# A gated recurrence's gate products: from fp32 to three passes over high and low parts, with the gate weights in the weight stream

## The chip, the core and the metric

One core of a Trainium2 chip runs the whole program. The metric is the device time of one execution in microseconds; the figure shown for a kernel is the median of several executions, and one more execution is recorded by the hardware profiler. TensorE (PE in the profile) multiplies, VectorE (DVE) and ScalarE (ACT) work element by element, GpSimd (POOL) does so too and here prepares weights, SyncE (SP) issues most of the DMA transfers.

## The reference, cut to what matters

One decoder layer on 1024 tokens and 1024 channels, in fp32. One of its three parallel branches is a gated linear recurrence on 1280 channels, with gate weights in 16 diagonal blocks of 80 × 80:

```
xa = causal_conv(lru_x, conv_w, conv_b)                   # 4 taps along the tokens
gate_a = sigmoid(einsum('bsni,nij->bsnj', xb, w_a) + b_a)   # xb: xa in 16 blocks of 80 channels
gate_x = sigmoid(einsum('bsni,nij->bsnj', xb, w_x) + b_x)
log_a = -8 * gate_a * softplus(-lam);  a = exp(log_a)
u = xa * gate_x * sqrt(1 - exp(2 * log_a))
h[t] = a[t] * h[t-1] + u[t]
o_a = (h * gelu(lru_y)) @ w_lru_o
```

`lru_x` and `lru_y` are columns of the projection of the normalized input. The other branches (a delta rule over 16 heads, and windowed attention), the merge and the FFN are not touched.

## The kernel before

Activations lie transposed in SBUF, 128 channels on the partitions and 1024 tokens along them. A dense product takes its weights as a stream of blocks of 128 × 1024 numbers. SP loads block n into one of two raw buffers (`load_block`), POOL splits it into a high part (a cast to fp32r, L241) and a low part (raw minus high, L243) in one of two pairs of buffers (`split_block`), and TensorE runs three fp32r products for each k tile and token half: high × high, high × low, low × high (`three_passes`, L251). The slot of a block is its number modulo 2. A load waits for the split of the block two before it, a split for the end of the dense product two before it. The result lands in one of two PSUM pairs, by the same slot. `Block(...).before` counts the blocks ahead, and the semaphores `s_wsplit` and `s_dense` count splits and products.

The recurrence stage takes 10 channel tiles in two turns of five. In a turn the stream has ten blocks in the order `LRU_ORDER`: x0, x1, y0, x2, y1, x3, y2, x4, y3, y4. After each y block the gates of tile j are multiplied (`lru_gates`): the 80-wide blocks do not line up with tiles of 128, so a tile needs the rows of its own tile and a halo of 64 rows from each neighbour (one neighbour only for tiles 0 and 4, so 64 rows). The gate weights are loaded piece by piece by SP (L554) into the tile `gw`, as they are, and TensorE multiplies them in fp32: for each of two gates and two token halves one product of the tile's own rows (L954) and one of the halo (L955), 8 in all, each of which the profile records as two. They go to PSUM banks 4 to 7.

ScalarE copies a finished x block out of PSUM (L1411), makes the halo copy from the neighbours (L1416, L1418; two buffers in turn), takes the GELU of the y block (L1423), two sigmoids (L1425, L1426), two exponentials (L1428, L1429) and a square root (L1431), and stores the output tile. VectorE's order is written by hand: convolution of tiles 0 and 1 (L1923, L1926), four modulation products, and then for each j the gated input (L1951 minimum, L1954 and L1957 products), the convolution of tile j + 2, the scan (L1963) with the product by the GELU (L1967), and four more modulation products up to j = 2. These modulation products (`later_ada`, L1936 and L1939) are a matrix-vector product that is needed later in the layer; its weights are loaded by SP (L575) in slices of 512 KB through two buffers, four slices behind each of the blocks y1, y2, y3 and y4. Every eight of them are summed over the partitions by TensorE inside block y2 and y4 (L975) and added by VectorE (L1946); the gates that use the same PSUM bank wait for that.

Of the kernel before, what the change touches and what calls it, by code (L numbers as in the profile page):

```python
# [54 lines left out]
LRU_AT = {key: c for c, key in enumerate(LRU_ORDER)}  # L55
MOD_SH1, MOD_SC1, MOD_G1, MOD_SH2, MOD_SC2, MOD_G2, MOD_N = range(0, 56, 8)
# [7 lines left out]
STREAM = [("lora", 1, 3), ("rwkv", PAIRS, 6), ("lru", LRU_T // LRU_G, 2 * LRU_G), ("att", 1, 12),  # L64
# [61 lines left out]
def build(nc, a, out):  # L126
    ctx = ExitStack()
    with ctx:
# [144 lines left out]
        def cols(w, c0, n):  # L273
            return w[:, bass.ds(c0, n)].rearrange("(k p) m -> p k m", p=P)
# [70 lines left out]
        def bank(B, n, rows=slice(0, P)):  # L345
# [31 lines left out]
                    ("gw", LRU_G * 4 * P), ("ada", 2 * 1024), ("acc", 1024), ("halo", 2 * T)])  # L377
        LRU_ARENA = 14 * T + 8 + 20 * P + 2048 + 1024
        halo = lr["halo"].rearrange("p (s n) -> p s n", s=2)
        HALO_DONE = (1, 3, 5, 7, 8)  # L380
        l_halo = made_by("act", "lru_halo_ready")
# [9 lines left out]
        ADA_BANK = [4, 2 * Block("lru", 2 * LRU_G - 2).slot]  # L391
        s_adb = [sem(f"later_ada_weights_loaded_{k}") for k in range(2)]
        l_ev, l_sa, l_rt, l_exp = made_by("act", "lru_block_evacuated", "lru_gates_ready", "lru_root_ready", "lru_decay_ready")
        l_pe, l_ada = made_by("pe", "lru_gates_done", "ada_sums_taken")
# [121 lines left out]
        def _(sp):  # L516
# [39 lines left out]
            with sp.Fori(0, TURNS["lru"]) as g:  # L556
                for c, (kind, j) in enumerate(LRU_ORDER):
                    load_block(sp, Block("lru", c, g), cols(w_in, (COL_LX if kind == "x" else COL_LY) + j * P + g * (LRU_G * P), P), P)
# [101 lines left out]
        def _(pool):  # L660
# [31 lines left out]
            split_turns("lru", [1024] * (2 * LRU_G))  # L692
# [22 lines left out]
        def _(pe):  # L715
# [225 lines left out]
            def lru_gates(g, j):  # L941

                pe.wait_ge(l_cv, upto(g * (4 * LRU_G) + 4 * min(j + 2, LRU_G)))
                pe.wait_ge(l_sa, upto(g * (2 * LRU_G) + 2 * j))
                pe.wait_ge(v_post, upto(PAIRS * POST))
                pe.wait_ge(ada_out, upto(g * ADA_U + (ADA_OUT0 + j // 2)))
                n = 2 * 16 * len(PIECES_OF[j])
                pe.wait_ge(s_gw[j], g * n + n)
                pe.wait_ge(l_halo, upto(g * HALO_DONE[-1] + HALO_DONE[j]))
                rows = slice(0 if j + 1 < LRU_G else 64, P if j > 0 else 64)  # L950
                for q in range(2):
                    for h in range(2):
                        hs = slice(h * 512, (h + 1) * 512)
                        mm(ps[:, 4 + 2 * q + h, :], gw[:, j, q, 0, :], xa_t[:, j, hs], start=True, stop=False)  # L954
                        ins = mm(ps[:, 4 + 2 * q + h, :], gw[rows, j, q, 1, :], halo[rows, j % 2, hs], start=False, stop=True)  # L955
                ins.then_inc(l_pe, 1)

            with pe.Fori(0, TURNS["lru"]) as g:
                for c, (kind, j) in enumerate(LRU_ORDER):
                    pe.wait_ge(l_ev, upto(g * len(LRU_ORDER) + max(c - 1, 0)))  # L960
                    if c == 0:
                        pe.wait_ge(ada_out, upto(g * ADA_U + ADA_OUT0))
                    if c == 1:
                        pe.wait_ge(a_gate, upto(PAIRS * 3))

                    def later_sums(k):

                        if k == 4:
                            pe.wait_ge(ada_acc, upto(g * ADA_G + (ADA_ACC0 + ADA_PHASE * j)))
                            if j == 2:  # L970
                                pe.wait_ge(l_sa, upto(g * (2 * LRU_G) + 2 * j))
                            else:
                                pe.wait_ge(l_ev, upto(g * len(LRU_ORDER) + c))
                            for q in range(8):
                                ins = mm(ps[:, ADA_BANK[j // 2 - 1], q:q + 1], ada_acc1[:, q * P:(q + 1) * P], ones[:, 0:1], start=True, stop=True)  # L975
                            ins.then_inc(l_ada, 1)
                    dense(pe, Block("lru", c, g), after=later_sums if kind == "y" and j in (2, 4) else None)
                    if kind == "y":
                        lru_gates(g, j)
# [299 lines left out]
        def _(act):  # L1279
# [122 lines left out]

            for g in range(TURNS["lru"]):
                for c, (kind, j) in enumerate(LRU_ORDER):
                    blk = Block("lru", c, g)
# [7 lines left out]
                    act.wait_ge(l_pe, upto(g * LRU_G + max(j - 1, 0)))  # L1413
                    act.wait_ge(l_cv, upto(g * (4 * LRU_G) + 4 * min(j + 2, LRU_G)))
# [9 lines left out]
                    act.wait_ge(l_pe, upto(g * LRU_G + (j + 1)))  # L1424
# [6 lines left out]
                    fn(lr["a2"], lr["a2"], ACT.Sqrt, scale=-1.0, bias=one_b).then_inc(l_rt, 1)  # L1431

# [229 lines left out]
        def _(dve):  # L1662
# [254 lines left out]
            def conv(g, j):  # L1917
# [4 lines left out]
                dve.wait_ge(l_pe, upto(g * LRU_G))  # L1922
# [35 lines left out]

            def recur(g, j):
# [11 lines left out]
            for g in range(TURNS["lru"]):  # L1971
                conv(g, 0)
                conv(g, 1)
                later_ada(g, 0)
                for j in range(LRU_G):
                    gated_input(g, j)
                    if j == 3:
                        later_ada_add(g, 1)
                    if j + 2 < LRU_G:
                        conv(g, j + 2)  # L1980
                    if g * LRU_G + j == LRU_T - 1:
                        dve.wait_ge(l_pe, upto(LRU_T))
# [271 lines left out]
```

## Time and profile before

| | us |
|---|---|
| median of 3 executions | 2933.76 (2930.98 to 2934.75) |
| the profiled execution | 2931.37 |
| its span, first to last instruction | 2929.4 |
| TensorE busy in the span | 2843.5 (97%) |
| VectorE, POOL, ScalarE busy | 1424.1, 752.5, 742.0 |
| mean granted TensorE clock | 0.992 of full speed |

A profile gives each instruction's start and duration on its engine, and what ended the idle time before it. Matmuls overlap, so the duration of one is longer than its step; steps are read from the chain. The times in the timelines count from the start of the span. A line number is that of kernel.py.

### The profile page before, as it was taken

To read this page: it belongs to the slowest core of one execution; us is meant where nothing else is said; L and a number is where in the kernel's file an instruction comes from. 1 tells how busy PE (TensorE), PEld (TensorE's weight loads), DVE (VectorE), ACT (ScalarE), POOL (GpSimd) and SP (SyncE) were. 2 spreads that over 40 slices of the span, in tenths; PEclk is the share of its full clock that TensorE was granted. 3 is DMA by queue.
4 is the path that set the end of the run, shared out by engine and by line. 5 is a ranking of instruction groups with operands and counts; after the bars stand their busy time and mean duration, and the time that the engine had idled before them with its cause. 6 is when DMAs were issued, how large, how long until landed. Compare 5 with 4: busy or idle time off the path is not lost.

```text
span 2929.4 us, 60683 instructions
## 1 busy us (share of the span) xinstructions
PE 2843.5 (97%) x25747; PEld 2350.4 (80%) x25747; DVE 1424.1 (49%) x1549; ACT 742.0 (25%) x1077; POOL 752.5 (26%) x490
## 2 busy tenths in 40 slices
PE   4999999999999999999999998999999999999999
PEld 3797979888888888867777776888888888888887
DVE  5645554546464545565654556566654222222223
ACT  4312121313131212144455666011122000000001
POOL 0403040303031212122222111333333333333332
PEclk9999999999999999999999999999999999999999
DMA  5201020202010111142431101476311111111112
GB/s 193 77 25 58 20 70 9 75 16 63 25 54 25 54 31 38 48 135 84 132 90 39 60 32 69 130 230 195 113 44 57 44 50 50 46 47 50 50 43 79
DMA packets 222611, 201.34 MB, mean 69 GB/s; under 512 B 22369, under 2 KB 193467, under 8 KB 222395
## 3 DMA queue, kind: packets, MB, share of 16 engines
q1 hardware_dynamic: 208928, 150.70, 17.1%
q10 hardware_dynamic: 13467, 47.31, 4.4%
q8 instruction: 191, 3.13, 0.4%
q14 instruction: 25, 0.20, 0.0%
HBM read 167.57 MB, written 30.41 MB: 68 GB/s over the span
## 4 chain that ended last, share of the span: by engine, by line
PE 94%; DVE 2%; issue 1%; ACT 1%; DMA 1%; SPq 0%; POOL 0%; ACTq 0%; DVEq 0%; POOLq 0%
PE ps L251 68%; PE ps L860 3%; PE ps L874 3%; PE ps L871 2%; PE ps L838 2%; PE ps L955 1%; PE ps L954 1%; PE ps L923 1%; PE ps L1049 1%; PE ps L828 1%; DMA arena<-in_w_ada 1%; PE ps L1074 1%; PE ps L1062 1%; PE ps L794 1%; PE ps L909 1%
## 5 line engine op out<-in xcount | busy, mean ns | idle before, releaser
L251 PE MATMUL ps<-x_hi,w_hi 128*128 128x512 f32 (+1 forms) x2576 | 835.2, 398 | 7.2 <-issue 4.1
L251 PE MATMUL ps<-x_lo,w_hi 128*128 128x512 f32 (+1 forms) x2576 | 815.6, 391 | 0.0
L251 PE MATMUL ps<-x_hi,w_lo 128*128 128x512 f32 (+1 forms) x2576 | 815.2, 391 | 0.0
L241 POOL CAST w_hi<-w_raw 128x1024 fp32r<-128x1024 f32 (+2 forms) x221 | 210.1, 951 | 2117.4 <-PE ps L251 1487.1
L251 PEld LDWEIGHTS ps<-x_hi,w_hi 128*128 128x128 f32 (+1 forms) x2576 | 477.9, 188 | 129.7 <-issue 30.7
L251 PEld LDWEIGHTS ps<-x_hi,w_lo 128*128 128x128 f32 (+1 forms) x2576 | 483.9, 188 | 104.7
L251 PEld LDWEIGHTS ps<-x_lo,w_hi 128*128 128x128 f32 (+1 forms) x2576 | 484.2, 188 | 100.8
L243 POOL TENSOR_TENSOR w_lo<-w_raw,w_hi 128x1024 fp32r<-128x1024 f32 (+2 forms) x221 | 484.0, 2190 | 17.7
L2203 DVE TENSOR_TENSOR arena<-ps,arena 128x1024 f32<-128x1024 f32 x21 | 25.7, 1225 | 376.5 <-PE ps L251 376.5
L251 PE MATMUL ps<-hid,w_hi 128*128 128x512 f32 x704 | 188.7, 390 | 0.0
L2221 DVE SCALAR_TENSOR_TENSOR arena<-ps,mod,arena 128x1024 f32<-128x1024 f32 x88 | 113.0, 1284 | 128.3 <-PE ps L251 128.2
L251 PEld LDWEIGHTS ps<-hid,w_hi 128*128 128x128 f32 x704 | 131.7, 188 | 27.0
L1868 DVE COPY_PREDICATED arena<-hid,ps 128x256 f32<-128x256 int32 x144 | 72.1, 501 | 137.7 <-PE ps L871 87.6
L1646 ACT ACTIVATE hid<-arena 128x1024 fp32r<-128x1024 f32 x22 | 23.4, 1062 | 442.0 <-PE ps L251 316.9
L251 PE MATMUL ps<-hid,w_lo 128*128 128x512 f32 x352 | 108.4, 389 | 0.0
L1497 ACT ACTIVATE arena<-arena 128x256 f32<-128x256 f32 x128 | 75.4, 590 | 80.5 <-DVE arena L2046 80.5
L874 PE MATMUL ps<-arena 64*64 64x64 f32 x2560 | 89.0, 218 | 0.0
L860 PE MATMUL ps<-arena 64*64 64x64 f32 x2560 | 84.1, 218 | 0.8
L874 PEld LDWEIGHTS ps<-arena 64*64 64x64 f32 x2560 | 83.0, 135 | 0.0
L860 PEld LDWEIGHTS ps<-arena 64*64 64x64 f32 x2560 | 79.9, 135 | 1.7 <-issue 1.7
L251 PEld LDWEIGHTS ps<-hid,w_lo 128*128 128x128 f32 x352 | 66.1, 188 | 13.8
L1765 DVE TENSOR_TENSOR arena<-arena 128x1024 f32<-128x1024 f32 (+1 forms) x27 | 41.8, 1548 | 72.6 <-ACT arena L1314 71.5
(289 smaller groups left out, 3449.2 us busy)
## 6 DMA issues: line engine op xcount, KB each, us to landing
w_raw<-in_w_in SPq DMA_DIRECT2D x78, 512.0 KB, 3.9
arena<-in_w_ada SPq DMA_DIRECT2D x48, 512.0 KB, 4.7
w_raw<-in_w_ffn_in SPq DMA_DIRECT2D x44, 512.0 KB, 3.7
arena<-gates_sig ACTq DMA_DIRECT2D x40, 512.0 KB, 4.2
gates_sig<-arena ACTq DMA_DIRECT2D x24, 512.0 KB, 2.7
w_raw<-in_w_ffn_out SPq DMA_DIRECT2D x22, 512.0 KB, 3.5
arena<-in_x SPq DMA_DIRECT2D x16, 512.0 KB, 6.9
y_a<-arena ACTq DMA_DIRECT2D x10, 512.0 KB, 2.6
```

The lines of the kernel that those rows point to most:

```text
L241: nc.gpsimd.tensor_copy(hi, raw).then_inc(s_whi, 1)
L243: nc.gpsimd.tensor_tensor(lo, raw, hi.bitcast(F32), ALU.subtract).then_inc(s_wsplit, 1)
L251: ins = nc.tensor.matmul(dst[h], wp, xp[h], start=first and m == 0, stop=last and m == 2)
L794: ins = mm(ps[hp, 4, c:c + 1], rw["bv"][hp, c * CHUNK:(c + 1) * CHUNK], ones[hp, 0:1], start=True, stop=True)
L838: ins = mm(dst, src[hp, c * CHUNK:(c + 1) * CHUNK], ar[hp, c, :, :], start=True, stop=True)
L860: ins = mm(bank(B, 2, hp)[:, c % BATCH, :], am[hp, c, AM_BA, :], xx[hp, 0, c, :], start=True, stop=True)
L871: ins = mm(bank(B, 0, hp)[:, c % BATCH, :], xx[hp, 1, c, :], y1[hp, c, :], start=True, stop=True)
L874: ins = mm(bank(B, 1, hp)[:, c % BATCH, :], y1[hp, c, :], xx[hp, 1, c, :], start=True, stop=True)
L1497: fn(sc[:, h, nn, :], sc[:, h, nn, :], ACT.Exp, bias=sm[:, SM_NEG, h, nn:nn + 1], scale=rq[:, gg % 2, t, n0 + nn, h:h + 1], accum_out=sm[: ...
L1765: v.tensor_tensor(dst, x0, x1, ALU.subtract).then_inc(v_mix, 1)
L1868: v.copy_predicated(blocks_of(xx[:, o, batch(B), :], lv, o), level_mask(lv, o), blocks_of(bank(B, o), lv, o)).then_inc(v_xu, 1)
L2221: v.scalar_tensor_tensor(r, ps[:, at:at + 2, :], mod[:, MOD_G2 + m:MOD_G2 + m + 1], r, ALU.mult, ALU.add).then_inc(m_dn, 1)
```

## The change

The gate products become three-pass products like the dense ones.

- The gate weights of a tile become blocks of the stream: one block of 512 columns behind each of y0 to y3, and two of 256 columns (gate a, gate x) behind y4, so that a turn has 16 blocks. POOL splits them from `gw` (`split_gates`). SP, in place of a load, waits until the block two before is split and then counts up the semaphore of the slot.
- The tile's own rows and its halo are each kept as a high part, made by ScalarE (`own_high`, and the lower halo rows in the loop), and a low part, made by VectorE (`low`). They lie in the four quarters of `hid`, the FFN's tensor, one set for all tiles. The arena loses its halo buffers.
- A gate product of a tile is 24 fp32r matmuls where it was 8 fp32 ones.
- As the slots of the stream shift, an x or y block can have the same PSUM pair as the block multiplied just before; it then waits for the copy of that block instead of the one before it.

```diff
+LRU_STREAM = [key for kind, j in LRU_ORDER
+              for key in [(kind, j)] + ([] if kind == "x" else [("gates", j)] if j + 1 < LRU_G else [("gate_a", j), ("gate_x", j)])]
+LRU_BLOCK = {key: c for c, key in enumerate(LRU_STREAM)}
...
+        own_hi, own_lo, halo_hi, halo_lo = (hid[:, k * T:(k + 1) * T] for k in range(4))
+        PARTS_DONE = (2, 5, 8, 11, 13)
...
+        def gates_before(g, j):
+            return lru_block("x", 0, g).before if j == 0 else lru_block("gates", j - 1, g).before + 1 if j < LRU_G else lru_block("gate_x", j - 1, g).before + 1
...
# SP
-                        sp.wait_ge(l_pe, upto(g * LRU_G))
+                        sp.wait_ge(s_dense, upto(gates_before(g, 0)))
                         wait_alone(sp)
                         load_gate_weights(g, j)
+                        for key in (("gates",) if j + 1 < LRU_G else ("gate_a", "gate_x")):
+                            blk = lru_block(key, j, g)
+                            sp.wait_ge(s_wsplit, upto(blk.before - 1))
+                            wait_alone(sp)
+                            sp.sem_inc(s_w[blk.slot], 16)
                     if c in (4, 6, 8, 9):
                         first = ADA_PHASE * (4, 6, 8, 9).index(c)
...
# POOL
+            def split_gates(g, key, j):
+                blk = lru_block(key, j, g)
+                q = slice(1, 2) if key == "gate_x" else slice(0, 1) if key == "gate_a" else slice(0, 2)
+                raw = gw[:, j, q, :, :].rearrange("p q h m -> p (q h m)")
+                hi, lo = (t[:, blk.slot, 0:raw.shape[1]] for t in (w_hi, w_lo))
+                n = 2 * 16 * len(PIECES_OF[j])
+                pool.wait_ge(s_gw[j], g * n + n)
+                pool.wait_ge(s_dense, upto(blk.before - 1))
+                wait_alone(pool)
+                nc.gpsimd.tensor_copy(hi, raw).then_inc(s_whi, 1)
+                pool.wait_ge(s_whi, upto(blk.before + 1))
+                nc.gpsimd.tensor_tensor(lo, raw, hi.bitcast(F32), ALU.subtract).then_inc(s_wsplit, 1)
...
# TensorE, lru_gates
-                pe.wait_ge(l_cv, upto(g * (4 * LRU_G) + 4 * min(j + 2, LRU_G)))
+                pe.wait_ge(l_low, upto(g * PARTS_DONE[-1] + PARTS_DONE[j]))
...
                 for q in range(2):
-                    for h in range(2):
-                        hs = slice(h * 512, (h + 1) * 512)
-                        mm(ps[:, 4 + 2 * q + h, :], gw[:, j, q, 0, :], xa_t[:, j, hs], start=True, stop=False)
-                        ins = mm(ps[:, 4 + 2 * q + h, :], gw[rows, j, q, 1, :], halo[rows, j % 2, hs], start=False, stop=True)
-                ins.then_inc(l_pe, 1)
+                    blk = lru_block("gates" if j + 1 < LRU_G else ("gate_a", "gate_x")[q], j, g)
+                    if j + 1 == LRU_G or q == 0:
+                        pe.wait_ge(s_wsplit, upto(blk.before + 1))
+                        wait_alone(pe)
+                    at = 0 if j + 1 == LRU_G else 2 * P * q
+                    dst = [ps[:, 4 + 2 * q + h, :] for h in range(2)]
+                    three_passes(dst, [t[:, blk.slot, at:at + P] for t in (w_hi, w_lo)], (both(own_hi), both(own_lo)), True, False)
+                    ins = three_passes(dst, [t[rows, blk.slot, at + P:at + 2 * P] for t in (w_hi, w_lo)], (both(halo_hi, rows), both(halo_lo, rows)), False, True)
...
-                    pe.wait_ge(l_ev, upto(g * len(LRU_ORDER) + max(c - 1, 0)))
+                    same = c > 0 and lru_block(*LRU_ORDER[c - 1]).slot == lru_block(kind, j).slot
+                    pe.wait_ge(l_ev, upto(g * len(LRU_ORDER) + (c if same else max(c - 1, 0))))
...
# ScalarE
+            def own_high(g, j):
+                act.wait_ge(s_dense, upto(gates_before(g, j)))
+                act.wait_ge(l_cv, upto(g * (4 * LRU_G) + 4 * (j + 1)))
+                fn(own_hi, xa_t[:, j, :], ACT.Copy).then_inc(l_high, 1)
+                if j > 0:
+                    fn(halo_hi[64:128, :], xa_t[64:128, j - 1, :], ACT.Copy).then_inc(l_high, 1)
...
                     if j + 1 < LRU_G:
-                        fn(halo[0:64, j % 2, :], xa_t[0:64, j + 1, :], ACT.Copy).then_inc(l_halo, 1)
-                    if j > 0:
-                        fn(halo[64:128, j % 2, :], xa_t[64:128, j - 1, :], ACT.Copy).then_inc(l_halo, 1)
+                        act.wait_ge(s_dense, upto(gates_before(g, j)))
+                        act.wait_ge(l_cv, upto(g * (4 * LRU_G) + 4 * (j + 2)))
+                        fn(halo_hi[0:64, :], xa_t[0:64, j + 1, :], ACT.Copy).then_inc(l_high, 1)
...
                     fn(lr["a2"], lr["a2"], ACT.Sqrt, scale=-1.0, bias=one_b).then_inc(l_rt, 1)
+                    if j + 1 < LRU_G:
+                        own_high(g, j + 1)
...
# VectorE
+            def low(g, j, part):
+                n = g * PARTS_DONE[-1] + (PARTS_DONE[j - 1] if j > 0 else 0) + (part if j > 0 else part // 2) + 1
+                hi, lo, rows, src = ((own_hi, own_lo, slice(0, P), j), (halo_hi, halo_lo, slice(64, P), j - 1), (halo_hi, halo_lo, slice(0, 64), j + 1))[part]
+                dve.wait_ge(l_high, upto(n))
+                v.tensor_tensor(lo[rows, :], xa_t[rows, src, :], hi[rows, :].bitcast(F32), ALU.subtract).then_inc(l_low, 1)
...
                 conv(g, 1)
+                low(g, 0, 0)
+                low(g, 0, 2)
                 later_ada(g, 0)
                 for j in range(LRU_G):
                     gated_input(g, j)
                     if j == 3:
                         later_ada_add(g, 1)
+                    if j + 1 < LRU_G:
+                        low(g, j + 1, 0)
+                        low(g, j + 1, 1)
                     if j + 2 < LRU_G:
                         conv(g, j + 2)
+                        low(g, j + 1, 2)
```

## Rows read from the trace of the kernel before

**Rows 1.** The page's chain that ended last, shares of the span by engine

```profile
PE 94%; DVE 2%; issue 1%; ACT 1%; DMA 1%; SPq 0%; POOL 0%; ACTq 0%; DVEq 0%; POOLq 0%
```

**Rows 2.** Windows: us; busy PE, PEld, DVE, ACT, POOL (instructions); clock; DMA; GB/s

```profile
1204.70:1516.98 312.28, 312.28 (x1245) 225.01 (x1241) 192.26 (x133) 141.62 (x126) 82.81 (x42) 1.00 0.36 111
```

**Rows 3.** Chain in order of time, first turn: start us, us, what

```profile
1216.78 32.66 PE ps L251 x144
1249.44 0.86 PE ps L954 x2
1250.30 1.05 PE ps L955 x2
...
1257.68 22.01 PE ps L251 x96
1279.69 0.86 PE ps L954 x2
...
1286.56 17.73 PE ps L251 x78
1304.29 1.68 PE ps L975 x16
```

**Rows 4.** Timeline of SP's DMA issues, first turn

```profile
1235.72 0.39 SPq L233 DMA_DIRECT2D w_raw<-in_w_in  x1
...
1241.93 8.11 SPq L575 DMA_DIRECT2D arena<-in_w_ada  x4
```

**Rows 5.** The modulation loads' line (L575), 1190 to 1540 us

```profile
DMA to landing us min/median/max: 3.3/3.9/5.8
```

**Rows 6.** Timeline of VectorE, modulation products before gates 0

```profile
1246.37 0.75 DVE L1936 TENSOR_SCALAR arena<-arena,mod 128x1024 f32<-128x1024 f32 x1
...
1250.73 4.80 DVE L1939 SCALAR_TENSOR_TENSOR arena<-arena,mod 128x1024 f32<-128x1024 f32 x2 [1.25 <-DMA arena<-in_w_ada]
```

**Rows 7.** Timeline of VectorE, between gates 0 and gates 1

```profile
1262.33 0.69 DVE L1951 TENSOR_SCALAR arena<-arena 128x1024 f32<-128x1024 f32 x1 [6.81 <-ACT arena L1428]
...
1270.76 5.94 DVE L1926 SCALAR_TENSOR_TENSOR arena<-arena,lru_par 128x1024 f32<-128x1024 f32 x3
1276.62 2.28 DVE L1963 TENSOR_TENSOR_SCAN arena<-arena 128x1024 f32<-128x1024 f32 x1
```

**Rows 8.** Timeline of ScalarE, GELU, table load and root of tile 0

```profile
1249.48 1.02 ACT L1423 ACTIVATE arena<-ps 128x1024 f32<-128x1024 f32 x1 [0.57 <-PE ps L251]
...
1263.36 1.28 ACT L1431 ACT_TABLE_LOAD   x1
1264.66 1.15 ACT L1431 ACTIVATE arena<-arena,bias_t 128x1024 f32<-128x1024 f32 x1
```

**Rows 9.** Timeline of POOL, the split of one whole block

```profile
1249.60 1.04 POOL L241 CAST w_hi<-w_raw 128x1024 fp32r<-128x1024 f32 x1 [6.88 <-issue]
1250.72 2.34 POOL L243 TENSOR_TENSOR w_lo<-w_raw,w_hi 128x1024 fp32r<-128x1024 f32 x1
```

**Rows 10.** Timeline of POOL, the split of the next turn's first block

```profile
1351.07 2.70 POOL L243 TENSOR_TENSOR w_lo<-w_raw,w_hi 128x1024 fp32r<-128x1024 f32 x1
```

**Rows 11.** Timeline of VectorE, the same stretch

```profile
1351.46 3.39 DVE L1954 TENSOR_TENSOR arena<-arena 128x1024 f32<-128x1024 f32 x1
```

**Rows 12.** One line: VectorE's convolution steps, ns min/median/max

```profile
L1926 DVE SCALAR_TENSOR_TENSOR arena<-arena,lru_par x30: 1283/1285/3304, 1229.8 to 1484.8; 128x1024 f32<-128x1024 f32 x30
```

**Rows 13.** One line: VectorE's low parts of the first stage

```profile
L1729 DVE TENSOR_TENSOR x_lo<-arena,x_hi x8: 1214/1215/1225, 48.7 to 72.4; 128x1024 fp32r<-128x1024 f32 x8
```

**Rows 14.** One line: ScalarE's high parts in the FFN

```profile
L1646 ACT ACTIVATE hid<-arena x22: 1057/1062/1063, 2228.0 to 2895.9; 128x1024 fp32r<-128x1024 f32 x22
```

**Rows 15.** Groups of POOL by form: xcount | busy us, mean ns

```profile
L243 POOL TENSOR_TENSOR w_lo<-w_raw,w_hi 128x512 fp32r<-128x512 f32 x56 | 73.0, 1304 | 4.5
```

**Rows 16.** Windows in the attention stage around an idle TensorE

```profile
1626.80:1629.80 3.00, 3.00 (x8) 1.94 (x6) 1.02 (x1) 2.97 (x10) 0.00 (x0) 0.50 0.00 0
```

**Rows 17.** Timeline of the kernel, 1300 to 1320 us

```profile
1308.87 0.17 DVE L1946 TENSOR_TENSOR mod<-ps,mod 128x8 f32<-128x8 f32 x1
```

More of the change, by code:

```diff
@@ L61 @@
 C_KEEP = C_ATT
-STREAM = [("lora", 1, 3), ("rwkv", PAIRS, 6), ("lru", LRU_T // LRU_G, 2 * LRU_G), ("att", 1, 12),
+STREAM = [("lora", 1, 3), ("rwkv", PAIRS, 6), ("lru", LRU_T // LRU_G, len(LRU_STREAM)), ("att", 1, 12),
           ("oa0", 4, 2), ("oa1", 4, 2), ("oa2", 4, 2), ("oc0", 4, 2), ("oc1", 4, 2), ("ob0", 4, 2), ("ob1", 4, 2),
@@ L376, in build, with lru_block @@
         lr = carve([("xp", T + 8), ("xa", LRU_G * T), ("ga", T), ("gx", T), ("aa", T), ("a2", T), ("gy", T), ("ya", T),
[L377 to L381, printed above, removed]
+                    ("gw", LRU_G * 4 * P), ("ada", 2 * 1024), ("acc", 1024)])
+        LRU_ARENA = 12 * T + 8 + 20 * P + 2048 + 1024
+        own_hi, own_lo, halo_hi, halo_lo = (hid[:, k * T:(k + 1) * T] for k in range(4))
+        PARTS_DONE = (2, 5, 8, 11, 13)
+        l_high, l_low = made_by("act", "lru_operand_high"), made_by("dve", "lru_operand_low")
+        def lru_block(kind, j, g=0):
+            return Block("lru", LRU_BLOCK[kind, j], g)
+        def gates_before(g, j):
+            return lru_block("x", 0, g).before if j == 0 else lru_block("gates", j - 1, g).before + 1 if j < LRU_G else lru_block("gate_x", j - 1, g).before + 1
         ada_w1 = lr["ada"].rearrange("p (s m) -> p s m", s=2)
@@ L390, in build @@
         ADA_U = ADA_G // KT
-        ADA_BANK = [4, 2 * Block("lru", 2 * LRU_G - 2).slot]
+        ADA_BANK = [4, 2 - 2 * lru_block("y", LRU_G - 1).slot]
         s_adb = [sem(f"later_ada_weights_loaded_{k}") for k in range(2)]
         l_ev, l_sa, l_rt, l_exp = made_by("act", "lru_block_evacuated", "lru_gates_ready", "lru_root_ready", "lru_decay_ready")
-        l_pe, l_ada = made_by("pe", "lru_gates_done", "ada_sums_taken")
+        l_ada = made_by("pe", "ada_sums_taken")
         l_cv, l_sq, l_u, l_out, l_z, gw_zero = made_by(
@@ L557, in _ @@
                 for c, (kind, j) in enumerate(LRU_ORDER):
-                    load_block(sp, Block("lru", c, g), cols(w_in, (COL_LX if kind == "x" else COL_LY) + j * P + g * (LRU_G * P), P), P)
+                    load_block(sp, lru_block(kind, j, g), cols(w_in, (COL_LX if kind == "x" else COL_LY) + j * P + g * (LRU_G * P), P), P)
                     if c == 1:
@@ L691, in _ @@
                         nc.gpsimd.tensor_copy(rw["xx"].rearrange("p (c n) -> p c n", n=CHUNK), eye.unsqueeze(1).broadcast_to([P, 2 * CHUNKS, CHUNK])).then_inc(x_id, 1)
-            split_turns("lru", [1024] * (2 * LRU_G))
+            def split_gates(g, key, j):
[10 more added lines that the diff above has]
+                nc.gpsimd.tensor_tensor(lo, raw, hi.bitcast(F32), ALU.subtract).then_inc(s_wsplit, 1)
+            with pool.Fori(0, TURNS["lru"]) as g:
+                for key, j in LRU_STREAM:
+                    if key in ("x", "y"):
+                        split_block(pool, lru_block(key, j, g), 1024)
+                    else:
+                        split_gates(g, key, j)
             for c in range(PER["att"]):
@@ L976, in later_sums @@
                             ins.then_inc(l_ada, 1)
-                    dense(pe, Block("lru", c, g), after=later_sums if kind == "y" and j in (2, 4) else None)
+                    dense(pe, lru_block(kind, j, g), after=later_sums if kind == "y" and j in (2, 4) else None)
                     if kind == "y":
@@ L1401, in store_y @@
                 act.dma_start(y_a[n * P:(n + 1) * P, :], lr["ya"]).then_inc(s_ya, 16)
+            def own_high(g, j):
[4 more added lines that the diff above has]
+                    fn(halo_hi[64:128, :], xa_t[64:128, j - 1, :], ACT.Copy).then_inc(l_high, 1)
             for g in range(TURNS["lru"]):
                 for c, (kind, j) in enumerate(LRU_ORDER):
-                    blk = Block("lru", c, g)
+                    blk = lru_block(kind, j, g)
                     lp = lambda row: lru_par[:, bass.ds(g * LRU_G + (row + j), 1)]
@@ L1978, in _ @@
                         later_ada_add(g, 1)
+                    if j + 1 < LRU_G:
+                        low(g, j + 1, 0)
+                        low(g, j + 1, 1)
                     if j + 2 < LRU_G:
                         conv(g, j + 2)
+                        low(g, j + 1, 2)
                     if g * LRU_G + j == LRU_T - 1:
-                        dve.wait_ge(l_pe, upto(LRU_T))
+                        dve.wait_ge(s_dense, upto(Block("att", 0).before))
                         for n in range(2):
```

14 lines of the change are left out of this document (7 added, 7 removed).

## Prediction

> **What bounds the kernel now.** I read the chain that ended last first: TensorE is 94% of it [rows 1]. The change touches only the recurrence stage, so next came the windows of that stage: from 1204.7 to 1517.0 TensorE is busy for all of 312.28 us, VectorE 192, POOL 83 [rows 2]. So one microsecond off the gates is one off the end, as long as nobody keeps TensorE waiting, and each new wait is paid in full. In the chain in order of time the reader is to see the cycle of a tile j: gates j, block x(j+2), block y(j+1), gates j+1, with no gap [rows 3]. Then the timelines of SP, VectorE, ScalarE and POOL inside one cycle show how early each input of the next gates is [rows 4 to 9]. That is where this change will be decided.
>
> **What TensorE saves.** The gates of a middle tile take 1286.56 − 1279.69 = 6.87 us; those of an end tile, where 64-row and 128-row products alternate, 1257.68 − 1249.44 = 8.24 (1.05 a step for 0.86) [rows 3]. Three-pass products go at 32.66/144 = 0.227 us in the blocks x0, x1, y0 [rows 3]. After: 24 of them, 5.44 us. An end tile changes between 64 and 128 rows 4 times instead of 8; at 0.19 each (taken from the fp32 row, from 0 to 0.4 if it is another price in this mode), 6.2. Also the two blocks behind fp32 gates take 22.01, where 96 × 0.227 = 21.77 [rows 3]; that 0.25 goes. A turn saves 3 × 1.43 + 2 × 2.04 + 5 × 0.25 = 9.6, two turns 19 us.
>
> **What is added elsewhere.** ScalarE: where it copied halo halves (1.06 a copy) it now makes high parts; the new one is a copy of the tile itself, 1.06 by the same form elsewhere [rows 14]. VectorE: two low parts for tile 0, three for 1 to 3, two for 4, a subtraction of the form that took 1.21 [rows 13]: 13 a turn, 16 us. POOL: six more splits a turn, the subtraction of 512 columns at 1.30 [rows 15] and a cast of half a whole one's, half that again for the last two. None of this is on TensorE, and VectorE has 120 us free. What counts is where the additions stand in its order.
>
> **Three dependencies that get longer.** (a) The gates now have one set of high and low tensors, so part j+1 is made only after gates j. (b) Blocks are split two ahead in a ring of two. With gate blocks in the ring, "two ahead" is less time. (c) SP waits, before it hands gate block j to POOL, for the split of the block two positions earlier, and everything behind it in SP's order waits too: the four modulation loads behind y1, y2, y3, y4. VectorE multiplies these in its fixed order before it starts on the gates' results.
>
> **Gates 1, worked through.** Before, SP issued the modulation loads at 1241.93 [rows 4], and the fourth product ended at 1250.73 + 4.80 = 1255.53 [rows 6], well before the exponential that releases VectorE at 1262.33 [rows 7, 8]. Now SP waits for the split of x2. This starts when y0 ends (1249.4) and takes 1.04 + 2.34 [rows 9] and some 0.2 of gaps: 1253.0, loads out from 1253.7. By the same 13.6 us from first issue to last product VectorE is free at 1267.3; as the loads go two in flight at 3.9 us (3.3 to 5.8) [rows 5] and POOL's split of y1 falls among the products, I take 1268.4. Without this, the earlier end of the gates would have released it at 1260.2. From there: minimum 0.7 [rows 7], a collision with POOL's subtraction for gate block 1 1.2, root 1.2 [rows 8], then product and two low parts at 1.2 each: 1275.2 (ScalarE's two copies behind the root keep pace). Convolution of x2: 0.8 + 3 × 1.28 without POOL [rows 12]; before, its three steps took 5.94 because the split of a whole block fell on them [rows 7]; now only the cast for x3 does, about 5.8: 1281.0. Copy on ScalarE 1.15: 1282.1. The last low part then meets POOL's subtraction for x3 and ends at 1284.5. TensorE, with gates 0 done at 1249.4 + 6.2 and 21.8 for two blocks, is ready at 1277.4. **Wait 7.1 us.**
>
> Collisions: while POOL subtracted from 1351.07 for 2.70 us, a VectorE product, 1.21 by the form of [rows 13], took 3.39 [rows 10, 11]; it ended 1.1 after POOL did. So each takes turns for a whole instruction. The Trainium skill, page "SBUF — State Buffer", section "Who interferes with whom", says the same of VectorE operations with two SBUF inputs: whoever issues first holds the port pair. By that rule the low parts, two SBUF inputs each, are among those that can be held up; if they were not, gates 1 would start near 1283.3. The trace has no subtraction into this tensor beside POOL.
>
> **The other waits of a turn.** Block x3 now has the PSUM pair that y1 has just left, so it waits for the GELU of y1, which waits for the output of tile 0: gates 1 start + scan 2.3 [rows 7] and product 1.2, store issue and gaps 0.5, table load 1.3 and GELU 1.0 [rows 8] = 6.3 against 5.44: **0.8**; the same behind gates 3, **0.8**. Gates 2: modulation loads leave at 1284, right after x3's split; the fourth product ends about 1297.5; then 6.1 to the end of two low parts (no collision this time), 6.4 of convolution (a gate block's split falls on it) and 2.5 of copy and low part give 1312.5 or a little more, and gates 2 also wait for the modulation sum, which VectorE adds after scan and product of tile 1: 1316.5 to 1317.5. TensorE is ready at 1314.2 (y2 holds the 1.68 of sums [rows 3]): **3.2**. Gates 3: loads wait for the split of x4, so for y2's end, then POOL collides with scan and product of tile 1; out at 1320.3, products done at 1335, then 16.5 as for gates 1: 1351.7 against 1344.6, **7.1**. Gates 4: low parts behind the modulation sum, **1.0** in two pieces. The next block: gate x alone lasts 3.1, a whole split 3.4 and its gaps start only when gate a is done and meet VectorE: **1.6**. Sum 7.1 + 0.8 + 3.2 + 7.1 + 0.8 + 1.0 + 1.6 = 21.6 a turn, 43.2 in two.
>
> **Sum.** 43.2 − 19 = +24. The profiled execution took 2931.4 (span 2929.4 and 2.0 around it): 2955.6. The median shown is 2.4 above it: 2958.
>
> **Clock.** Behind idle time of 1.9 us in the attention stage TensorE ran at a granted 0.50 (1.2 GHz, not 2.4) for the 3 us from 1626.8 [rows 16]. Waits of 7 us will do this too: four in all, each costing half of 3 us or a little more, 6 to 7 together. The gates after a wait are slower then, but in the cycle behind gates 1 VectorE is held by the loads (1297.5) and not by the exponential (1294.6), and the PSUM wait of 0.8 is absorbed. I take 0 for it, up to +7. The Trainium skill, page "TensorE: Matmul & The Clock Gate", section "HAM oscillation — how this bites in real kernels", has waits re-throttle the array each time; by it the sum would be the upper one.
>
> **Rivals.**
> 1. The forecast: loads late and parts late, 2958. If nothing collides with POOL and loads land at 3.3, gates 1 and 3 start 3 us sooner, four times: −12, 2946; if they land at 5.8 and the clock costs 7, +13, 2971. Chance 0.78.
> 2. Larger still: each late load also pushes the next whole cycle, so the waits do not stay at 7 but grow as the weight loads queue behind them; 8 waits with 2 us more, 2972 or more. Against it: SP issued the load of y1 at 1235.7 for a block that began at 1268 [rows 4], and a load that goes 10 us later still comes in time. Chance 0.09.
> 3. The modulation data is there in time (SP's wait passes early, or VectorE's products fit in). Then VectorE starts at 1260.2, conv(x2) at 1267.6 when its block is copied, last low part by 1276, in front of 1277.4. Waits left: 0.8 + 3.2 + 0.8 + 1.0 + 1.6 = 7.4 a turn, 15 in all: −4, 2930. It decides if the loads go out before 1246. The order in the code and the ring speak against it. Chance 0.08.
> 4. Everything hidden, the other side: 2934 − 19 = 2915. The mechanism is the shorter gates alone, decisive if each part is ready within the 21.8 us of two blocks. For it: before, no gates waited. Against: VectorE's add for gates 2 was done at 1309.0 for a start at 1310.2 [rows 17], and 5 us of work moves in front of it. Chance 0.05.
>
> **Range and chances.** A difference under 0.2% (5.9 us) can't be told from none. Rival 1 is slower throughout its range; rival 3 lies within 0.2% mostly, with a third of it faster. Slower 0.87, same 0.06, faster 0.07. The range leaves out rivals 3 and 4 and most of 2: 2943 to 2972.
>
> **What would show it.** Right: gates start-to-start cycles of about 35 us for 30; TensorE idle before gates 1 and 3 ended by VectorE's low-part subtraction; SP's modulation loads at 1253 and not at 1242; products ending near 1268; gates of 5.4 us; conv of x2 at 1275. The modulation step is wrong if those loads leave before 1246, the collisions if conv takes 4.7 throughout, the saving if 24 gate products take other than 5.4 us at full clock. The prediction falls if gates 1 start by 1278.

## The result, and the profile after

| | before | after |
|---|---|---|
| median of 4 executions each, us | 2932.61 (2930.98 to 2934.75) | 2952.59 (2951.24 to 2957.77) |
| ratio of after to before, 95% interval | | 1.0077 (1.0064 to 1.0089) |
| the profiled execution, us | 2931.37 | 2951.54 (span 2949.7) |
| TensorE busy in the span, us | 2843.5 | 2835.1 |
| mean granted TensorE clock | 0.992 | 0.987 |

The kernel is 20 us slower. TensorE is busy for 8 us less and still ends 20 later, and the page's chain that ended last shows where the rest went (it was 94% TensorE, [rows 1]):

```profile
PE 89%; DVE 4%; DMA 2%; issue 2%; ACT 1%; POOL 1%; SPq 0%; ACTq 0%; POOLq 0%; DVEq 0%
```

To compare kernels I use one measure from here on, called the stage: from the first matmul of block x0 to the first transpose of the attention stage, both from TensorE's timeline. Before it lasts 1216.53 to 1527.94, 311.4 us, and TensorE is busy in all of it. After, the windows view (columns as in [rows 2]) says this of it, and of the 9 us behind the start of gates 1:

```profile
1215.38:1548.30 332.92, 304.05 (x1316) 245.58 (x1314) 217.47 (x163) 156.49 (x141) 110.48 (x66) 0.95 0.34 104
```
```profile
1283.20:1286.00 2.80, 2.77 (x7) 2.22 (x8) 2.77 (x2) 0.00 (x0) 0.00 (x0) 0.50 0.95 323
1286.00:1289.00 3.00, 3.00 (x9) 2.33 (x8) 2.69 (x3) 2.35 (x3) 0.00 (x0) 0.57 0.58 221
1289.00:1292.00 3.00, 3.00 (x15) 2.45 (x14) 0.49 (x2) 1.74 (x2) 0.38 (x1) 1.00 0.78 224
```

The stage is 21.5 us longer, which is the whole difference. It holds 332.92 − 304.05 = 28.9 us in which TensorE is idle, and its granted clock is 0.95 where it was 1.00: right behind the wait at gates 1 it is 0.50 (1.2 GHz) and comes back to 2.4 GHz some 5 us later. TensorE's timeline, first turn, has every wait with what ended it in brackets:

```profile
1283.23 2.04 PE L255 MATMUL ps<-hid,w_hi 128*128 128x512 f32 x4 [6.86 <-DVE hid L2017]
...
1315.51 1.17 PE L255 MATMUL ps<-hid,w_hi 128*128 128x512 f32 x4 [0.44 <-DVE mod L1998]
...
1350.00 2.05 PE L255 MATMUL ps<-hid,w_hi 128*128 128x512 f32 x4 [7.03 <-DVE hid L2017]
...
1373.56 1.16 PE L255 MATMUL ps<-hid,w_hi 128*128 128x512 f32 x4 [0.55 <-POOL w_lo L722]
...
1376.93 0.50 PE L255 MATMUL ps<-x_hi,w_hi 128*128 128x512 f32 x1 [0.16 <-POOL w_lo L247]
```

These are gates 1, 2, 3, the second half of gates 4, and the next block: 15.0 us in this turn, 13.8 in the second. L2017 is the low-part subtraction, L1998 the modulation sum. The reader is also to see the first column of durations: four matmuls take 2.04 at gates 1 and 3 and 1.17 at gates 2, the clock again.

Back from gates 1 along the inputs, first SP's queue (answers to [rows 4]: the modulation loads, there at 1241.93):

```profile
1235.78 4.41 SPq L237 DMA_DIRECT2D w_raw<-in_w_in  x2
...
1252.41 8.17 SPq L593 DMA_DIRECT2D arena<-in_w_ada  x4
```

then VectorE (to [rows 6, 7]): modulation products, minimum, low parts, convolution of x2, last low part.

```profile
1256.48 2.15 DVE L1988 TENSOR_SCALAR arena<-arena,mod 128x1024 f32<-128x1024 f32 x1 [10.00 <-DMA arena<-in_w_ada]
...
1266.05 1.29 DVE L1991 SCALAR_TENSOR_TENSOR arena<-arena,mod 128x1024 f32<-128x1024 f32 x1 [2.14 <-DMA arena<-in_w_ada]
1267.27 1.78 DVE L2003 TENSOR_SCALAR arena<-arena 128x1024 f32<-128x1024 f32 x1
...
1271.49 2.47 DVE L2017 TENSOR_TENSOR hid<-arena,hid 128x1024 fp32r<-128x1024 f32 x2
...
1274.84 4.58 DVE L1978 SCALAR_TENSOR_TENSOR arena<-arena,lru_par 128x1024 f32<-128x1024 f32 x3
1280.61 2.10 DVE L2017 TENSOR_TENSOR hid<-arena,hid 64x1024 fp32r<-64x1024 f32 x1 [1.18 <-ACT hid L1468]
```

and POOL's subtraction for block x3, beside that last low part:

```profile
1278.42 3.20 POOL L247 TENSOR_TENSOR w_lo<-w_raw,w_hi 128x1024 fp32r<-128x1024 f32 x1
```

The 64-row low part takes 2.10 us and ends 1.09 after POOL does; where nothing runs beside it, it takes 1.22 (below). VectorE sat 10.00 us before the first modulation product, for the load.

### The profile page after: what moved, and what is told of

Read it like the earlier page. It is cut to its first block, busy times and chain, and to the rows that moved or that the text cites. A ratio compares the mean times of both kernels' runs of the same rounds, so it can differ in the third digit from the quotient of the medians.

```text
span 2949.7 us, 60983 instructions
## 1 busy us (share of the span) xinstructions
PE 2835.1 (96%) x25827; PEld 2371.9 (80%) x25827; DVE 1449.8 (49%) x1575; ACT 752.0 (25%) x1087; POOL 782.2 (27%) x514
## 4 chain that ended last, share of the span: by engine, by line
PE 89%; DVE 4%; DMA 2%; issue 2%; ACT 1%; POOL 1%; SPq 0%; ACTq 0%; POOLq 0%; DVEq 0%
PE ps L255 66%; PE ps L897 3%; PE ps L911 3%; DMA arena<-in_w_ada 2%; PE ps L908 2%; PE ps L875 2%; PE ps L960 1%; PE ps L1091 1%; PE ps L865 1%; PE ps L1116 1%; PE ps L1104 1%; DVE arena L1978 1%; PE ps L831 1%; DVE hid L2017 1%; PE ps L917 1%
## 5 line engine op out<-in xcount | busy, mean ns | idle before, releaser
L255 PE MATMUL ps<-hid,w_hi 128*128 128x512 f32 (+1 forms) x864 | 239.7, 400 | 28.5 <-DVE hid L2017 26.6
L255 PEld LDWEIGHTS ps<-hid,w_hi 128*128 128x128 f32 (+1 forms) x864 | 164.5, 193 | 69.0 <-issue 35.3
L255 PE MATMUL ps<-hid,w_lo 128*128 128x512 f32 (+1 forms) x432 | 135.7, 396 | 0.0
L255 PEld LDWEIGHTS ps<-hid,w_lo 128*128 128x128 f32 (+1 forms) x432 | 82.8, 192 | 17.8
```

The lines of the kernel that those rows point to most:

```text
L255: ins = nc.tensor.matmul(dst[h], wp, xp[h], start=first and m == 0, stop=last and m == 2)
```

## Experiments

Every ratio is to executions of the kernel before on the same chip: their median was 2934.0 beside e1 to e4, 2934.2 beside e5 to e7 and 2933.1 beside e10 and e11. The stage and its idle time are from each kernel's own trace, so from one execution; that of e1 was the longest of its ten (2940.5), that of e3 the shortest of its four (2943.0). What a kernel differs from before by its stage and by its medians agrees within some 5 us.

| kernel | median us | ratio to before, 95% interval | stage us | TensorE idle in it | clock in it |
|---|---|---|---|---|---|
| before | 2932.6 | | 311.4 | 0 | 1.00 |
| after | 2952.6 | 1.0077 (1.0064 to 1.0089) | 332.9 | 28.9 | 0.95 |
| e1_loads_first | 2932.4 | 0.9996 (0.9987 to 1.0006) | 314.9 | 11.0 | 0.97 |
| e2_late_loads_only | 2938.8 | 1.0021 (1.0011 to 1.003) | 317.3 | 5.5 | 1.00 |
| e3_no_low_parts | 2948.0 | 1.0054 (1.0035 to 1.0072) | 324.5 | 19.3 | 0.97 |
| e4_gates_short_only | 2917.1 | 0.9937 (0.9916 to 0.9959) | 293.9 | 0 | 1.00 |
| e5_early_sum | 2925.7 | 0.9978 (0.9967 to 0.999) | 307.4 | 6.4 | 0.98 |
| e6_early_sum_ring4 | 2921.8 | 0.9958 (0.9946 to 0.997) | 298.3 | 2.7 | 1.00 |
| e7_clock_kept | 2950.1 | 1.0056 (1.0035 to 1.0076) | 331.9 | 10.9 | 1.00 |
| e10_before_new_order | 2931.8 | 0.9996 (0.9986 to 1.0005) | 311.4 | 0 | 1.00 |
| e11_ring4_only | 2949.8 | 1.0058 (1.0041 to 1.0075) | 329.6 | 22.4 | 0.96 |

**Loads first: is it SP's order?** In the kernel after, SP's hand-over of the gate block, with its wait for the split of the block two positions earlier, moves behind the four modulation loads. Nothing else changes.

```diff
                         load_gate_weights(g, j)
-                        for key in (("gates",) if j + 1 < LRU_G else ("gate_a", "gate_x")):
-                            blk = lru_block(key, j, g)
-                            sp.wait_ge(s_wsplit, upto(blk.before - 1))
-                            wait_alone(sp)
-                            sp.sem_inc(s_w[blk.slot], 16)
                     if c in (4, 6, 8, 9):
...
                             sp.dma_start(ada_w1[:, n % 2, :], src).then_inc(s_adb[n % 2], 16)
+                    if kind == "y":
+                        for key in (("gates",) if j + 1 < LRU_G else ("gate_a", "gate_x")):
+                            blk = lru_block(key, j, g)
+                            sp.wait_ge(s_wsplit, upto(blk.before - 1))
+                            wait_alone(sp)
+                            sp.sem_inc(s_w[blk.slot], 16)
```

> The changed kernel with one edit: SP issues the four modulation loads behind y1 to y4 before it waits for the split of the block two ahead of the gate block, not behind that wait. Theory (late modulation loads cost most of the waits): first loads of a turn leave near 1241 to 1247 and not 1252, the wait before gates 1 (6.9 us in the changed kernel) is gone, the one before gates 3 (7.0) falls by half or more, and the time falls by 12 to 18 us, to about 2937. Rival A (the low parts and POOL's splits are what is late, the loads only share the blame): the waits stay at 4 us and more, 2948. Rival B (nothing but the loads was late): the whole 19 us that TensorE saves appears, 2915.

Measured: 2932.4, level with before, where I had expected 2937; by the medians the 20 us are gone, in the stage 18.0 of the 21.5. The loads leave at

```profile
1252.30 7.88 SPq L588 DMA_DIRECT2D arena<-in_w_ada  x4
```

in a trace in which x0 starts 5.7 later than in that of after (1221.09 for 1215.38), so 5.8 us earlier in the stage. The waits of 6 to 7 us at gates 1 and 3 are gone. What is left, from TensorE's timeline:

```profile
1314.60 1.51 PE L255 MATMUL ps<-hid,w_hi 128*128 128x512 f32 x4 [3.29 <-DVE mod L1999]
...
1358.11 2.04 PE L1018 MATMUL ps<-keep,arena 128*128 128x1 f32 x15 [1.94 <-DVE arena L1992]
```

Gates 2 wait for the modulation sum, and TensorE's sums for the last modulation product. So first loads that leave 5.8 us later cost 18 us of stage, because four cycles are hit. All of that is idle time (28.9 us for 11.0); TensorE's busy time is the same in both (304.05 and 303.96), so the slow clock has no part in the difference.

The loads are not back where they were before. They leave 37.0 us behind x0 after, 31.2 in e1 and 25.4 before. Of the 5.8 that are left, 5.2 are in the load of block y1, which stands ahead of them in SP's queue: it goes out 24.4 us behind x0 in both new kernels and 19.2 before. In e1 it goes out at 1245.50, just behind POOL's split of gate block 0 (1243.96 + 1.30): the ring of two, point (b) of the prediction.

**Late loads alone: is it enough?** The kernel before, with one wait in SP's order ahead of the modulation loads, for the split of the block just issued, so that they leave at about the time they do after.

```diff
                     if c in (4, 6, 8, 9):
                         first = ADA_PHASE * (4, 6, 8, 9).index(c)
+                        sp.wait_ge(s_wsplit, upto(Block("lru", c, g).before + 1))
+                        wait_alone(sp)
```

> The kernel before, with fp32 gates, and one wait more: SP lets the modulation loads behind y1 to y4 go only when that block itself is split, which is the moment at which the changed kernel lets them go. Theory: the late loads alone make VectorE late; gates 1 start 1 to 3 us late, the stage grows by 8 to 15 us, 2941 to 2948. Rival A (loads are hidden when there are no low parts behind them): no change, 2933.

Measured: 2938.8, and loads at 1253.21, 36.9 us behind x0 as in the kernel after. I had expected a wait at gates 1 and 8 to 15 us of stage; it is 5.9. There are waits at gates 2 only, 2.9 and 2.6 us in the two turns; gates 1 and 3 do not wait:

```profile
1312.82 1.12 PE L956 MATMUL ps<-arena 128*128 128x512 f32 x2 [2.87 <-DVE mod L1948]
```

Loads that are 11.5 us later than before cost 5.9 us of stage where nothing else is longer; with the rest of the change, the last 5.8 of them alone cost 18 (e1). The lateness needs the rest of the change beside it. My reading is that low parts, shorter gates and late loads eat from the same slack; no run has late loads and short gates without the other additions.

**No low parts.** The kernel after, with no low-part subtraction on VectorE; the gates use the high part in its place, with the same 24 products.

```diff
-                pe.wait_ge(l_low, upto(g * PARTS_DONE[-1] + PARTS_DONE[j]))
+                pe.wait_ge(l_high, upto(g * PARTS_DONE[-1] + PARTS_DONE[j]))
...
-                    three_passes(dst, [t[:, blk.slot, at:at + P] for t in (w_hi, w_lo)], (both(own_hi), both(own_lo)), True, False)
...
+                    three_passes(dst, [t[:, blk.slot, at:at + P] for t in (w_hi, w_lo)], (both(own_hi), both(own_hi)), True, False)
...
-                    if j + 1 < LRU_G:
-                        low(g, j + 1, 0)
-                        low(g, j + 1, 1)
```

> The changed kernel without VectorE's low-part subtractions: TensorE multiplies the high part where it would multiply the low part, with the same number of products, so the output lacks the low parts. Loads stay late. Theory: 2.5 us before the convolution and 2.1 to 3.3 behind it leave the path to gates 1 and 3, the waits there fall from 7 to about 4, 2941 to 2944. Rival B (loads are the whole cause): the waits stay, within 3 us of the changed kernel, 2950. Rival A (low parts are the whole cause): waits gone, 2915 to 2920.

Measured: 2948.0. The waits at gates 1 and 3, 6.0 to 7.0 us after, fall to some 4.2 as expected, and end on ScalarE's high halo part (behind the same convolution). The time did not fall as expected (2941 to 2944). The stage gives 8.4 us back, somewhat under half of what the loads gave in e1 (18.0); by the medians it is 4.6 of 20. So the low parts are an addition to a chain that is late already, worth 5 to 8 us.

**Gates short, nothing else.** The kernel before; its gate products become 24 three-pass ones on operands that lie there anyway (lg0 by x), so that nobody has anything more to prepare.

```diff
+                part = lambda t, r: [t[r, 0, h * 512:(h + 1) * 512] for h in range(2)]
...
-                        mm(ps[:, 4 + 2 * q + h, :], gw[:, j, q, 0, :], xa_t[:, j, hs], start=True, stop=False)
-                        ins = mm(ps[:, 4 + 2 * q + h, :], gw[rows, j, q, 1, :], halo[rows, j % 2, hs], start=False, stop=True)
...
+                    three_passes(dst, [lg0_hi, lg0_lo], (part(x_hi, whole), part(x_lo, whole)), True, False)
+                    ins = three_passes(dst, [lg0_hi[rows, :], lg0_lo[rows, :]], (part(x_hi, rows), part(x_lo, rows)), False, True)
```

> The kernel before, with its gates as 24 three-pass products whose operands are tensors that lie ready (a weight tensor of the stage before, the first tile of the input), so the gate values are not those of the reference; all waits and copies are those of before. It measures what TensorE saves by itself. Theory: 5.4 us for a middle tile, 6.2 for an end tile, 19 us less in all, 2914. Rival (a shorter gate alone already uncovers a wait, as VectorE's modulation sum for gates 2 had only 1.2 us to spare): 2917 to 2922.

Measured: 2917.1; the stage falls by 17.5 us without a wait. The time is that of my rival, but not for its reason: nothing was uncovered, the saving was smaller. That is the most that the change could have brought.

**The order of VectorE and the buffers.** e5 is e1, and VectorE takes the first modulation sum before the scan of tile 1 rather than behind it. e6 is e5 with four buffers for the modulation weights where there were two (two semaphores of the first stage are counted on for the two new ones).

```diff
+                    if j == 1:
+                        later_ada_add(g, 0)
                     recur(g, j)
-                    if j == 1:
-                        later_ada_add(g, 0)
...
-                            sp.wait_ge(ada_acc, upto(g * ADA_G + (ADA_ACC0 + n - 1)))
+                            sp.wait_ge(ada_acc, upto(g * ADA_G + (ADA_ACC0 + n - 3)))
...
-                            sp.dma_start(ada_w1[:, n % 2, :], src).then_inc(s_adb[n % 2], 16)
+                            sp.dma_start(ada_w1[:, n % 4, :], src).then_inc(s_adb[n % 4], 16)
```

> The kernel after with SyncE's loop of hand-over waits behind the modulation loads, and VectorE's modulation sum and next products ahead of the scan of the block, not behind it. Loads_first alone stood at 2932.4 us (ratio 0.9996), with a wait of 3.3 us at gates 2 that ended on the modulation sum. If that wait is VectorE's order of work alone, it goes (3.3 us in each turn) and this kernel stands 2 to 6 us under loads_first, 2926 to 2930. If it is the ring of two loads that limits, the wait moves to the next low parts or to the sum's taking by TensorE, at the same total: 2930 to 2935. My estimate is the second: the products wait for loads that are issued only as their buffers come free.

> As early_sum, with four buffers in place of two for the modulation weights, so that loads run four products ahead. If loads paced by two buffers are what is left of the waits, the idle time of TensorE in the stage falls from 11 us (loads_first) to under 6, with the slow clock that follows each stop, and the time is 2920 to 2928 us, under both kernels. If VectorE's own work is what paces, it stays at 2930 to 2935.

Measured: e5 2925.7, e6 2921.8. For e5 I had taken the second reading (the wait only moves) and was wrong: the wait at gates 2 is gone, and the sums wait 1.7 and 1.5, much as in e1 (1.9 and 1.4). e6 came out as its first reading said: idle time 2.7 us, clock 1.00 for the stage. It stands 12 us under the kernel before on the same chip. Its stage, and its last low part before gates 1, at 1.22 us with nothing of POOL's beside it:

```profile
1215.79:1514.04 298.25, 295.52 (x1315) 239.60 (x1314) 229.92 (x163) 156.47 (x141) 120.39 (x66) 1.00 0.37 116
```
```profile
1273.88 1.22 DVE L2019 TENSOR_TENSOR hid<-arena,hid 64x1024 fp32r<-64x1024 f32 x1 [1.19 <-ACT hid L1470]
```

**The same order, without the change.** e10 is the kernel before with e6's four buffers and early sum.

> The kernel before, with what early_sum_ring4 adds to VectorE's and SyncE's side: four buffers for the modulation weights and the first modulation sum ahead of the scan. The gate products stay fp32. It tells whether the 12 us that early_sum_ring4 stands under before come from the change or from the schedule alone. In the trace of before TensorE doesn't wait for the modulation in this stage, so I expect no change: 2931 to 2937 us, ratio 0.999 to 1.001. Rival: the earlier loads and sum give something on their own; then it is under 2928, and the change itself is worth less than the two together.

Measured: 2931.8, stage 311.4 as before. The new order is worth nothing by itself, since no wait was there to remove; e6's gain is the change's own.

**Four buffers alone.** e11 is the kernel after with the four buffers, SP's order and the sum left as they are.

> The kernel after with four buffers in place of two for the modulation weights, and nothing else: SyncE's loads still stand behind its wait for the split of the gate weights, and the sum stands where it was. If the place in SyncE's queue is the cause of the waits of 6 to 7 us at gates 1 and 3, the loads still leave at about 1252; what four buffers save is the pacing between them (products end at about 1263 in place of 1267), so the waits fall to 3 or 4 us and the time to 2938 to 2945. If the two buffers were the cause, it stands where early_sum_ring4 does, 2919 to 2925. If neither, at 2950 to 2955.

Measured: 2949.8. The wait at gates 1 fell more than I had written, the total less: it is 0.2 us short of my third case, "neither". TensorE's timeline of the first turn:

```profile
1276.91 1.15 PE L255 MATMUL ps<-hid,w_hi 128*128 128x512 f32 x4 [1.39 <-DVE hid L2018]
...
1311.76 1.91 PE L255 MATMUL ps<-hid,w_hi 128*128 128x512 f32 x4 [4.38 <-DVE mod L1999]
...
1357.88 1.44 PE L1018 MATMUL ps<-keep,arena 128*128 128x1 f32 x6 [3.81 <-DVE arena L1992]
```

The loads still leave at 1251.55 but all within 2.4 us; gates 1 wait 1.4 for 6.9, gates 2 wait 4.4 for 0.4, gates 3 not at all for 7.0, and the sums 3.8 for none. A wait taken away at one place came back at the next. e6 has these four buffers and no such waits, but two things more, SP's order and the early sum; no run parts those two with four buffers.

**The clock.** e7 is the kernel after with 26 more fp32r products ahead of TensorE's wait at gates 1 and 3, into a bank that nobody reads then; they fill the wait.

```diff
+                pe.wait_ge(l_sa, upto(g * (2 * LRU_G) + 2 * j))
+                if j in (1, 3):
+                    for _ in range(26):
+                        mm(ps[:, 7, :], lg0_hi, x_hi[:, 0, 0:512], start=True, stop=True)
                 pe.wait_ge(l_low, upto(g * PARTS_DONE[-1] + PARTS_DONE[j]))
-                pe.wait_ge(l_sa, upto(g * (2 * LRU_G) + 2 * j))
```

> The kernel after, with 26 extra fp32r products of 128x512 (lg0 high by the high part of x, into a bank that nobody reads then) ahead of TensorE's wait for the low parts at gates 1 and gates 3. They fill some 5.9 us of waits of 6.0 to 7.0 and change nothing that anyone waits for. Theory: the stop costs twice, once as the wait and once as the clock of 0.50 behind it; with the engine busy in the wait, gates 1 and 3 take 5.4 us in place of 8.1, so up to 4 x 2.6 = 10 us off: 2943 us, ratio to before 1.003 to 1.004. Rival: what comes behind gates 1 and 3 waits for VectorE all the same, so that most of it is given back as longer waits at gates 2 and at the sums: 2949 to 2953. I expect 2944 to 2947.

Measured: 2950.1. The clock stays at 1.00 and gates 1 take 5.7 us in place of 8.1, but the total is near that of after, as the rival said and against my own 2944 to 2947:

```profile
1281.24 1.17 PE L255 MATMUL ps<-hid,w_hi 128*128 128x512 f32 x4 [0.25 <-DVE hid L2020]
...
1287.36 0.72 PE L255 MATMUL ps<-x_hi,w_hi 128*128 128x512 f32 x2 [0.40 <-ACT arena L1476]
...
1312.64 1.16 PE L255 MATMUL ps<-hid,w_hi 128*128 128x512 f32 x4 [1.39 <-DVE mod L2001]
...
1348.35 0.93 PE L255 MATMUL ps<-hid,w_hi 128*128 128x512 f32 x3 [2.36 <-DVE hid L2020]
```

Counted from x0's start, gates 2 begin 1.6 us earlier than after and gates 3 only 0.4 (98.5 for 100.1, 134.3 for 134.6). TensorE arrives sooner and waits longer. The 0.40 at block x3 is the PSUM wait of the prediction, which the slow gates of the kernel after had covered.

## Why the prediction held, step by step

The forecast was +24 us and 2958; measured +20.0 and 2952.6. In the stage: forecast −19.2 + 43.2 = +24.0; measured +21.5. It comes apart as follows, e6 giving the busy time of the same products at full clock (295.5): saving 311.4 − 295.5 = 15.9; slow clock 304.05 − 295.5 = 8.5; idle 28.9; −15.9 + 8.5 + 28.9 = +21.5. So the direction and the cause were right. The total is nearer than its terms: the long waits came 1.8 us under the forecast and the small ones 12.6, the clock 8.5 over and the saving 3.3 short. That these leave 2.5 us is in part luck.

- **The chain to gates 1.** x0 starts 1.15 us earlier in the trace of after (1215.38 for 1216.53), so 1.15 is added to compare. Loads leave: forecast 1253.7, measured 1253.6. VectorE free: 1268.4, measured 1268.4. Two low parts done: 1275.2, measured 1275.1. Convolution done: 1281.0, measured 1280.6. Last low part: 1284.5, measured 1283.9, the gates 0.5 behind it. TensorE ready: 1277.4, measured 1277.5. Wait: 7.1, measured 6.9. Gates 3: start 1351.7, measured 1351.2; wait 7.1, measured 7.0. Second turn 6.0 and 6.8. These terms carry the forecast, and e1 shows that the loads' place behind SP's hand-over is what makes them: with that alone undone, the waits at gates 1 and 3 are gone and the time is that of before.
- **The small waits (7.4 a turn)** came to 1.2 in the first turn and 1.1 in the second. These are the terms most off. Gates 2 start at 1316.7 in the terms of before, forecast 1316.5 to 1317.5, so VectorE's side was right; but TensorE, held by slow gates 1, was ready only 0.4 ahead, not 3.2. The PSUM waits of 0.8 are covered in the same way. e7, where the clock is kept, tells how much the slow gates covered: there the small waits are 3.6 and 3.5 us, so 4.8 of the 12.6. The other 7.8 were too much in any case: gates 2 wait 1.4 in e7 for 3.2, the PSUM pairs 0.40 for 0.8. The next block waited 0.16 and 0.20 for 1.6: I put the splits of the two half blocks too close to it. With the long ones, 26.6 for 28.4, the waits came to 28.9 in two turns, not 43.2.
- **The clock, taken at 0 with up to +7,** cost 8.5 of TensorE's busy time. As an entry of the sum it was mis-sized, but the reason given for 0 (VectorE is held anyway, so slower gates are absorbed) holds for most of it: e7 takes the slow clock away and gets 1.0 us of stage back, as the waits grow by almost as much (by the medians 2.5, from ranges that touch). So part of "clock 8.5" and of "small waits 12.6 less than forecast" are the same microseconds: the forecast counted the small waits at full clock and the clock at nothing, and each is off in part by what the other covers. The rule cited from the Trainium skill, page "TensorE: Matmul & The Clock Gate", section "HAM oscillation — how this bites in real kernels", is borne out as far as the clock goes: it fell at each of the four long waits. Its consequence for the time, the upper sum, is not.
- **The saving, 19,** was 15.9 in the full change and 17.5 with products alone (e4). Gates 0 took 6.21 (forecast 6.2), middle gates 5.4 at full clock. The 0.25 for each of ten changes of mode is what isn't there: 17.5 less the 16.7 of the gates leaves 0.8 for all ten. The prediction had read 22.01 for the two blocks behind gates 0, where rows change between 64 and 128; behind gates 2 the chain of before has 21.81. The other 1.6 between e4 and e6 lies in pieces of 0.06 to 0.2 at gates 1, 3 and 4 and in the blocks behind them (gates 1 take 5.50 us in e6 and 5.44 in e4).
- **Collisions.** The last low part took 2.10 beside POOL's subtraction and 1.22 without. The minimum took 1.78 beside the one for gate block 1 and 0.69 in e1, where it comes elsewhere. The rule of the Trainium skill, page "SBUF — State Buffer", section "Who interferes with whom", held for a subtraction that writes hid: it ended 1.09 us after POOL's, as the product of [rows 11] did (1.1). In both, POOL had started first.
- **Rivals.** The larger one (2972 or more) did not come: waits do not grow from cycle to cycle. The third (modulation data in time, 2930) did not come either; e1 comes near it at 2932.4, with loads that leave at 1247.7 in the terms of before and 11.0 us of waits for 15. The fourth (2915, everything hidden) is what e4 shows for the gates alone at 2917.1; e6 comes to 2921.8.

Open: how much of after's wait at gates 1 goes to each collision by itself, as no run removes POOL's split alone. Also open are the 5.2 us by which the load of y1 goes out late in both new kernels, as no run has a longer ring; and two sets of high and low parts, so that tile j+1's are made a tile earlier, weren't tried.

## What to carry to other kernels

A wait put in a queue is a wait for everything behind it: before pricing "SP waits for the split", list the loads issued after it and who consumes them. Here moving four loads of each group ahead of a hand-over was worth 20 us, and turned a change that costs 0.8% into one that, with the sum taken earlier and two more buffers, brings 0.4%. And when the engine that sets the end gets shorter work, re-time all its suppliers; taking one wait away (e11, e7) mostly uncovers the next.

## What the runs showed of the hardware

The length of a wait didn't decide what the clock did. In the stage of e5, a wait of 1.45 us ahead of the sums was followed by full clock for 2 us and 0.54 in the next 2, while TensorE was busy throughout:

```profile
1495.40:1497.40 2.00, 1.97 (x17) 1.97 (x18) 1.85 (x3) 1.39 (x2) 0.00 (x0) 1.00 0.00 0
1497.40:1499.40 2.00, 2.00 (x6) 1.57 (x7) 2.00 (x3) 1.76 (x2) 0.00 (x0) 0.54 0.00 0
```

In e11, a wait of 1.39 us ahead of gates 1 was followed by 1.00 in both stretches:

```profile
1276.90:1279.00 2.10, 2.09 (x9) 1.78 (x10) 2.06 (x2) 0.00 (x0) 2.10 (x1) 1.00 0.00 0
1279.00:1281.00 2.00, 2.00 (x10) 1.65 (x9) 1.59 (x1) 0.00 (x0) 1.92 (x2) 1.00 0.00 0
```

and in e2, whose gate products are fp32, a wait of 2.87 us was followed by 1.00 in each 2 us up to 1320.8. The low clock can also come some 2 us after the wait is over, so it is to be looked for behind the next group of products and not only at the wait.
